# Picking the first four experts' tokens in two halves of 64 slots

## The reference, cut to what matters

```python
expert_idx = g_idx * EXPERTS_PER_GROUP + local          # 2 of 32 experts for each token
xs = concatenate([ht, zeros])[slot_tok]                 # tokens gathered to expert slots
def expert_block(args):
    xb, e = args
    return (silu(xb @ e_gate[e]) * (xb @ e_up[e])) @ e_down[e]
contrib = ys[dest] * wts                                # weighted and added back to the tokens
```

## Time and profile before

| | |
|---|---|
| median of 3 runs | 1900.11 us (1898.47 to 1901.05) |
| the profiled execution's own time | 1910.55 us |
| its span in the profile | 1908.7 us |
| mean granted PE clock | 0.898 of full speed |
| PE busy, share of the span | 1556.5 us, 82% |
| DMA, chain that ended last | 38% of the span |

### The profile page before, as it was taken

One profiled execution on the slowest core, in us unless ns is written; L12 is line 12 of the kernel. 1 busy time (PEld: TensorE's weight loads), 2 busy tenths in 40 slices (PEclk: granted clock), 3 DMA queues, 4 the chain that ended last, 5 costly groups with the idle time before them and its releaser, 6 DMA issues.

```text
span 1908.7 us, 29538 instructions
## 1 busy us (share of the span) xinstructions
PE 1556.5 (82%) x11778; PEld 842.5 (44%) x11778; DVE 763.4 (40%) x1694; ACT 351.2 (18%) x777; POOL 135.7 (7%) x170
## 2 busy tenths in 40 slices
PE   5999999997767777677889999998796776677785
PEld 2764543534433433334366554353453343333442
DVE  0253566767222221122535356576732221222226
ACT  0235321221101111010222532121211111011011
POOL 3000013104000000000020000220200000000000
PEclk7899999998988888888989899899878888888888
DMA  9353437537899999999945443754659999999994
GB/s 333 138 183 139 138 115 214 192 129 294 341 427 427 429 429 429 429 429 427 395 175 211 147 122 122 210 170 167 287 209 427 427 429 429 429 429 429 428 428 185
DMA packets 93544, 567.54 MB, mean 297 GB/s; under 512 B 7126, under 2 KB 7998, under 8 KB 68115
## 3 DMA queue, kind: packets, MB, share of 16 engines
q1 hardware_dynamic: 81682, 532.05, 68.6%
q0 software_dynamic: 11776, 34.33, 6.4%
HBM read 550.53 MB, written 15.81 MB: 297 GB/s over the span
## 4 chain that ended last, share of the span: by engine, by line
PE 49%; DMA 38%; DVE 6%; issue 2%; ACT 2%; SPq 1%; DVEq 1%; PEldq 0%; ACTq 0%; PEld 0%
DMA ring<-in_exp_w_up 36%; PE ps L1491 10%; PE ps L970 9%; PE ps L995 8%; PE ps L1217 2%; PE ps L1352 2%; DMA ring<-in_w_ada 2%; PE ps L834 2%; PE ps L977 2%; PE ps L1466 2%; PE ps L892 1%; PE ps L1186 1%; PE ps L1162 1%; SPq L613 1%; SPq L607 1%
## 5 line engine op out<-in xcount | busy, mean ns | idle before, releaser
L1491 PE MATMUL ps<-ring,xTb 128*32 128x256 f32 x4224 | 328.9, 480 | 228.8 <-DMA ring<-in_exp_w_up 223.6
L1491 PEld LDWEIGHTS ps<-ring,xTb 128*32 128x32 f32 x4224 | 162.4, 137 | 395.0 <-issue 351.1
L2655 DVE TENSOR_TENSOR hb<-sg,ps 128x128 f32<-128x128 f32 x66 | 25.0, 379 | 474.1 <-ACT sg L1861 474.1
L995 PE MATMUL ps<-ring,hT 128*128 128x512 f32 x384 | 171.4, 598 | 0.0
L1466 PE MATMUL ps<-sel,h_tm 128*128 128x128 f32 (+1 forms) x912 | 169.4, 314 | 0.0
L970 PE MATMUL ps<-hT,ring 128*128 128x288 f32 x640 | 165.1, 417 | 4.7 <-DVE hT L2018 2.5
L1466 PEld LDWEIGHTS ps<-sel,h_tm 128*128 128x128 f32 x912 | 129.6, 195 | 55.3 <-issue 29.5
L970 PEld LDWEIGHTS ps<-hT,ring 128*128 128x128 f32 x640 | 122.5, 194 | 42.8 <-issue 7.6
L1505 PE MATMUL ps<-ring,hTb 128*32 128x256 f32 x2112 | 128.9, 385 | 2.5 <-DVEq L2658 2.5
L1861 ACT ACTIVATE sg<-ps 128x128 f32<-128x128 f32 x66 | 18.3, 277 | 595.2 <-PE ps L1491 595.2
L2663 DVE COPY ys<-ps 32x256 f32<-32x256 f32 x124 | 52.6, 424 | 159.1 <-PE ps L1505 157.9
(11 more groups left out here) (482 smaller groups left out, 1695.9 us busy)
## 6 DMA issues: line engine op xcount, KB each, us to landing
ring<-in_exp_w_gate SPq DMA_DIRECT2D x66, 2048.0 KB, 18.8
ring<-in_exp_w_up SPq DMA_DIRECT2D x66, 2048.0 KB, 23.3
ring<-in_exp_w_down SPq DMA_DIRECT2D x66, 2048.0 KB, 24.7
ring<-in_w_ada SPq DMA_DIRECT2D x24, 2048.0 KB, 10.3
ring<-in_w_in SPq DMA_DIRECT2D x22, 2048.0 KB, 8.9
ring<-in_w_out SPq DMA_DIRECT2D x8, 2048.0 KB, 9.2
h0s<-in_state_ssd POOLq DMA_DIRECT2D x16, 512.0 KB, 7.1
out_ssd_s<-h0s POOLq DMA_DIRECT2D x16, 512.0 KB, 5.2
```

The costliest lines, as they stand in the source:

```text
L995: last = mm(o[:, :], hT[:, k, T0[i]:T0[i] + P], w[:, k, :], start=(k == 0), stop=(k == KT - 1))
L1491: last = mm(ps[32 * j:32 * j + 32, b, 0:2 * P], xTb[:, k, m * BLK:(m + 1) * BLK], w[:, 0:2, k * D_EXPERT + j * P:k * D_EXPERT + (j + 1) * ...
```

## The change

PE gathers the first quad in two halves of 64 slots. The first half (slots 0 to 63, experts 0 and 1; all 8 blocks of k, 64 columns each, bank 6) comes before the stage, the second (slots 64 to 127, bank 7) right after the first expert's `gate_up`, ahead of `rows_of` and `down`. ACT copies each half into its columns of `xTb` (`take_first`). The first quad's `gate_up` of expert 0 waits for the first copy alone, that of expert 2 for the second. The next quad's gather then has no place after expert 0; it is done after expert 1 (4 blocks of k), 2 and 3 (2 blocks each). DVE's `select` for the next quad, which overwrites `sel`, moves behind `hidden` of expert 0 and waits for the second half. ACT's first quad is written out ahead of its loop. The other quads are as before.

```diff
-        g_half = sem("gather_half_taken")
+        g_half = sig("gather_half_taken", QUADS + 1)
...
-                def gather(lo, hi, n):
+                def gather(lo, hi, n, at=0):
                     for k in range(lo, hi):
-                        o = ps[:, 6 + k * n // 512, k * n % 512:k * n % 512 + n]
+                        o = ps[:, 6 + (at + k * n) // 512, (at + k * n) % 512:(at + k * n) % 512 + n]
+                        c = at // KT
                         for i in range(NT):
-                            ... sel[0:ROWS[i], i, 0:n],
+                            ... sel[0:ROWS[i], i, c:c + n],
...
-                gather(0, 4, QS).then_inc(gq_full.sem, 1)
-                gather(4, 8, QS).then_inc(gq_full.sem, 1)
+                gather(0, KT, 2 * BLK).then_inc(gq_full.sem, 1)
...  PE, quad(Q, first)
+                    if first:
+                        pe.wait_ge(g_half.sem, g_half.at(l, 1))
+                    else:
+                        pe.wait_ge(g_taken, steady + Q + 1)
                     for m in range(QUAD):
+                        if first and m == 2:
+                            pe.wait_ge(g_taken, steady + Q + 1)
                         gate_up(d, b, m)
                         if m == 0:
                             if first:
+                                gather(0, KT, 2 * BLK, CH).then_inc(gq_full.sem, 1)
                                 ... rows_of x3
+                        if m == first:
                             pe.wait_ge(sel_ready, steady + Q + 2)
-                        last = gather(2 * m, 2 * m + 2, QS)
+                        if not first:
+                            last = gather(2 * m, 2 * m + 2, QS)
+                        elif m:
+                            last = gather((0, 0, 4, 6)[m], (0, 4, 6, 8)[m], QS)
                         ...
                         down(d, b)
...  ACT
+                def take_first(half):
+                    act.wait_ge(gq_full.sem, gq_full.at(l, 1 + half))
+                    cp(xTb[:, :, 2 * BLK * half:2 * BLK * (half + 1)], ps[:, 6 + half, :]...)
+                take_first(0)              # ahead of quad 0
                         silu(d, b)
+                        if first and m == 0:
+                            take_first(1)
...  DVE, quad(Q, first)
-                    select(QS, QS)
+                    if not first:
+                        select(QS, QS)
                         hidden(d, b)
                         if m == 0:
                             if first:
+                                dve.wait_ge(gq_full.sem, gq_full.at(l, 2))
+                                select(QS, QS)
                                 dve.wait_ge(drow_full.sem, drow_full.at(l, 1))
```

More of the change, by code:

```diff
@@ L1459, in _ @@
                 keep_clock(2)
-                def gather(lo, hi, n):
+                def gather(lo, hi, n, at=0):
                     for k in range(lo, hi):
-                        o = ps[:, 6 + k * n // 512, k * n % 512:k * n % 512 + n]
+                        o = ps[:, 6 + (at + k * n) // 512, (at + k * n) % 512:(at + k * n) % 512 + n]
+                        c = at // KT
                         for i in range(NT):
-                            last = mm(o, h_tm[0:ROWS[i], i, k * P:(k + 1) * P], sel[0:ROWS[i], i, 0:n],
+                            last = mm(o, h_tm[0:ROWS[i], i, k * P:(k + 1) * P], sel[0:ROWS[i], i, c:c + n],
                                       start=(i == 0), stop=(i == NT - 1))
@@ L1530, in quad @@
                     d0 = pe.snap(pairs + 2 * Q)
-                    pe.wait_ge(g_taken, steady + Q + 1)
+                    if first:
+                        pe.wait_ge(g_half.sem, g_half.at(l, 1))
+                        idle["pe"].stand(pe)
+                    else:
+                        pe.wait_ge(g_taken, steady + Q + 1)
                     for m in range(QUAD):
                         d, b = d0 + m // 2, m % 2
+                        if first and m == 2:
+                            pe.wait_ge(g_taken, steady + Q + 1)
+                            idle["pe"].stand(pe)
                         gate_up(d, b, m)
@@ L1849, in take_gather @@
                     cp(xTb[:, 4 * half:4 * half + 4, :], ps[:, 6 + half, :].rearrange("p (k t) -> p k t", k=4)
-                       ).then_inc(g_taken if half else g_half, 1)
+                       ).then_inc(g_taken if half else g_half.sem, 1)
+                def take_first(half):
+                    act.wait_ge(gq_full.sem, gq_full.at(l, 1 + half))
+                    cp(xTb[:, :, 2 * BLK * half:2 * BLK * (half + 1)], ps[:, 6 + half, :].rearrange("p (k t) -> p k t", k=KT)
+                       ).then_inc(g_taken if half else g_half.sem, 1)
                 tb = act.snap(before)
                 pairs = act.snap(tb + l * STEADY)
[L1854 to L1857, removed]
+                take_first(0)
                 def silu(d, b):
@@ L1867, in take_down, with quad @@
                     last.then_inc(ysa, 1)
-                with act.Fori(0, QUADS) as Q:
+                def quad(Q, first):
                     d0 = act.snap(pairs + 2 * Q)
@@ L1879, in _ @@
                         take_down(d, b, m)
+                quad(0, True)
+                with act.Fori(1, QUADS) as Q:
+                    quad(Q, False)
                 act.wait_ge(plan_ready.sem, plan_ready.at(l, 1))
@@ L2648, in _ @@
                 spreads = dve.snap(tb + l * QUADS)
-                dve.wait_ge(gq_full.sem, gq_full.at(l, 2))
-                idle["dve"].stand(dve)
                 def hidden(d, b):
@@ L2693, in quad @@
                             if first:
+                                dve.wait_ge(gq_full.sem, gq_full.at(l, 2))
+                                idle["dve"].stand(dve)
+                                select(QS, QS)
                                 dve.wait_ge(drow_full.sem, drow_full.at(l, 1))
```

## The result

The changed kernel takes 1924.81 us (1920.40 to 1925.58, 4 runs) against 1899.29 us (1895.62 to 1901.05, 4 runs) for the kernel before: 1.0123 times as long, 95% interval 1.0091 to 1.0155. The sign was forecast, the size was not: +25.5 us where +14 stood, outside the range. Of the runs of the kernel before that were taken later, beside the experiments, one at 2472.34 us was in a slower state and is left out.

A forecast was written before the change was run, and what follows sets the result against it. The DMA weight stream was taken to bound both expert stages. Layer 0 +8.0 and layer 1 +3.6 gave +11.6 us (1911.7 on the median), or +16.0 at full clock (1916.1); forecast 1914 us, range 1899.5 to 1922.

The forecast's parts named there:

- The path: Both expert stages: DMA is full at 428 GB/s, so only the stream's start and its dry time move the end.
- Part 1: First gather with 64 columns: 7.6 us instead of 8.44 at full clock; 13.2 instead of 14.70 at half clock.
- Part 2: Clock falls 5.1 us into the 64-column gather; gather costs 1.85 and gate_up 1.9 more, so the stream starts 2.9 us later.
- Part 3: Second half between gate_up and down: down issue late, DMA dry 4.9 us, plus 0.2 us at the next expert, each layer.
- The sum: Whole kernel: +11.6 us as profiled or +16.0 with both first gathers at full clock; 1914 us said.
- My case of full clock in both layers: Both first gathers at full clock in the timed runs: 2 x 8.0 = +16.0 us, 1916.1 us.
- Layer 1 as profiled: Layer 1 with its first gather at half clock before: 1.5 us saved, 4.9 and 0.2 lost, +3.6 us.
- the midpoint between the two cases: Half clock as profiled (1911.7 us on the median) and full clock (1916.1) taken as about equally likely: 1914 us.
- Part 4: Next quad's gather, second copy's wait, xTb writes and DVE's queue: covered by other work, costing nothing.
- A: Rival: the clock holds in the 64-column gathers; -1.2 or -0.5 us, 1899 to 1900 us, no change; chance 0.13.
- B: Rival: columns set the gather's time at half clock, 7.4 us in layer 1; -6.9 us, 1893 us; chance 0.04.
- C: Rival: DVE's chain behind the second half becomes the wait; 1 to 4 us a layer more, about 1920 us; chance 0.05.

The follow-up runs named there:

- b_extra: Kernel before, with a repeated 128-column gather of all 128 slots (48 records) behind the first gate_up of a layer: 1908.02 us, 1.0027 times before.
- x_late: Changed kernel, with the second half gathered after the second expert's gate_up and the next quad's gather behind experts 2 and 3: 1906.71 us, 1.0022 times before.
- b_same: Kernel before, unchanged, timed again with a second profile: 1900.93 us; the profiled execution took 1896.63 us.
- x_hold: Changed kernel, with four 512-column identity matmuls as fillers in each of the two 64-column gathers: 1913.91 us.
- a_again: Changed kernel, unchanged, timed again with a second profile: 1921.26 us, 1.0103 times before.
- the three with bank 6: One filler matmul in the last pair's wait, overwriting the running sum, in the changed kernel, kernel before and late-second-half version: 1889.83, 1877.50, 1877.39 us, none comparable.
- after: Changed kernel as first measured and profiled, against the kernel before: 1924.81 us, 1.0123 times before.
- x_down_first: Changed kernel, with the first expert's down placed ahead of the second half's gather: 1919.34 us, 1.0089 times before.
- a_fill0: Changed kernel, with one 512-column filler matmul into free bank 0 in the last pair's wait of each layer: 1918.77 us, 1.0074 times before.
- x_late_hold: Changed kernel, with the second half after the second gate_up and four filler matmuls in each 64-column gather: 1907.80 us, 1.0023 times before.
- b_fill0: Kernel before, with one 512-column filler matmul into bank 0 in the last pair's wait of each layer: 1907.26 us, 1.0010 times before.

## Why the prediction was right and wrong

**The path: right.** The stream's start and its dry time set when the stream ends; both stages run at 428 GB/s behind them. In layer 0 of `b_extra` and `x_late` they account for the whole difference from `b_same` (3.5 of 3.5 us, 3.4 of 3.7).

**Part 1, the 64-column gather: right.** In `x_hold` 12 records at full clock take 1.86 us as a piece, 1.79 from one start to the next, so 7.2 to 7.4 for 48, where 7.6 stood. At half clock I put 13.2; 12.99 was measured.

**Part 2, the fall: right, size near.** The idle rule of the Trainium skill, "TensorE: Matmul & The Clock Gate", Part 1, would have kept the clock, since PE is busy without a gap. The trace goes against it: the fall is there in both layer-0 gathers of the change, and `x_hold` removes it. It came 4.1 to 4.3 us into the first gather of layer 0, in all eight profiles without fillers in it, and not 5.1 us in (the middle of my own bounds, 3.3 and 7.6, would have been 5.45). The gather took 10.42 us, 9.4 forecast. Against `b_same` the first gate issue is 3.4 us late in layer 0 (2.9 forecast).

**Part 3, the dry stream: right.** Down issue 15.3 us behind the gate issue (15.2), 5.3 and 5.5 us dry (5.1). "The end of this stall isn't given back" holds too; that nothing comes on top of it, behind the stream, did not.

**The sum: this is what failed, in two steps.** Between `b_same` and `a_again` lie 25.0 us of span:

| us | layer 0 | layer 1 | forecast, a layer |
|---|---|---|---|
| later first gate issue | 3.4 | 3.3 | 2.9 |
| dry | 5.3 | 5.4 | 5.1 |
| rest, behind the stream | 5.0 | 0.7 | none |
| ahead of the stage | 1.9 | | none |

The larger step: no term stood for the clock behind the stream. I took the rest of the stage and what follows as fixed ("with their lengths unchanged"). In layer 0 the last pair fell in clock and cost 5.0 us; in layer 1 the last `gate_up` fell, 5.24 us in `a_again` and 6.55 in the first profile instead of 3.66. My case of full clock in both layers gave +16.0 where 23.1 came, and 5.7 of the 7.1 between them are this. The 1.9 us ahead of the stage belong to no change of code, so they are chance between two profiles.

The smaller step: "Layer 1 as profiled: -1.5 + 4.9 + 0.2 = +3.6", and the midpoint between the two cases, which took 2 us off. The base was not an even choice: 63 of 100 runs of before are in the lower group, and the 1899.29 of the comparison lies in it. Where layer 1's gather is at full clock before, the stream starts 3.3 us later there (`a_again`) or 6.4 (the first profile) instead of 1.5 sooner. I had seen the 7.9 us between the layers and the 11 us between profile and median, and still took half of it.

**Part 4: right.** No wait on DVE or on the second copy shows on the chain. Rivals A, B and C didn't come about: the clock fell, the columns don't set the time at half clock (12.99, not 7.4), and the down issue of expert 1 comes 5.9 us behind its gate issue, where 6.1 was allowed for.

**Open: why the last pair falls.** The record shows more than chance here. In layer 1 the last `gate_up` took 4.93 to 6.55 us in the five profiles in which PE had waited 2.5 to 4.3 us for its weights, and 3.66 in the eight in which it had waited 1.9 us or less (the three with bank 6 left out). All five are versions with a delayed issue (`after`, `a_again`, `x_hold`, `b_extra`, `x_down_first`); of the six such versions only `a_fill0` escapes. In layer 0 the last pair fell in the two profiles with 2.3 and 2.6 us of that wait and no filler, and in none of those with 1.5 or less. So the late stream seems to cost twice, once in itself and once as a longer idle wait behind which the clock falls. No experiment varied that wait by itself, and two falls had another place: `x_late_hold` fell in layer 1's last pair after only 0.62 us of it, and `a_fill0` fell behind its filler. Of the 25.5 us, what the two profiles of the change differ by (3.8 us, layer 1's first gather at 12.99 or 10.42) is open too. A 14.70 us gather stands in the profile of before at 1910.55 and in that of `b_fill0` at 1907.87; for the other runs of the upper group it is inferred.

## What to carry to other kernels

Where a transfer queue is issued from the ends of compute steps, count the bytes in flight at each issue and the time to the next one. What may be put between two issues is what those bytes cover, here about 11 us, and moving one issue forward can starve the next. A stream that ends later also lengthens the waits of the compute engine for the last pieces, and the clock may fall there: leave room for it in the range. Halving the columns of a matmul that its weight loads already fill saves a tenth and can cost the clock, which then makes the next steps dearer as well. And if a profiled run is far from the median, take the forecast's base from the median's side, and widen the range by what two profiles of one kernel may differ by, here 14 us.

## What the runs showed of the hardware

- The clock fell while PE was busy without a gap: the gather of 48 records, 64 columns each behind 128-column weight loads, had 1.00 and then 0.50 in layer 0 in each of eight profiles, and took 10.42 us instead of about 7.4. Four 512-column calls in it (0.96 us each) held the clock at 1.00 (`x_hold`).
- One 512-column call in a wait of 1.06 us kept the clock for the groups right behind it (10.7 us instead of 16.0, `a_fill0`), but a fall followed 16 us later; layer 0 gained 3.5 us.
- The last `gate_up` of layer 1 took 3.66 us after waits of up to 1.9 us and 4.93 to 6.55 us after waits of 2.5 to 4.3 us (13 profiles).
- 100 timed runs of the kernel before, on one core of each of four chips, spread over 21 us (1892.7 to 1913.8).
